# Splitting the pair's combine around the activation transposes, and two neighbouring rows of w_down to a partition

## What is computed

```
gates = softmax over the top 4 of 32 router logits, 0 elsewhere
for each expert e:
    hdn = x @ w_up[e] + b_up[e]                   # 1024 -> 2048
    gt  = min(hdn[:, :1024], 7)
    up  = clip(hdn[:, 1024:], -7, 7)
    act = (up + 1) * gt * sigmoid(1.702 * gt)
    acc += gate[:, e] * (act @ w_down[e] + b_down[e])   # 1024 -> 1024
h = h + acc
```

## Time and profile before

| | us |
|---|---|
| median of 3 runs | 1397.82 |
| lowest, highest | 1396.66, 1398.46 |
| span of the profiled execution, first to last instruction | 1394.0 |
| PE busy in it | 1257.9 |
| the 33 expert passes, from 246.7 to 1300.6 and the last one behind it | to about 1337 |

### The profile page before, as it was taken

How to read it: one execution, slowest core, us unless ns; L and a number is a source line. 1 busy time by engine, 2 the same in 40 slices (tenths; PEclk the granted TensorE clock), 3 DMA queues, 4 the chain that set the end, 5 groups by cost and what they waited for, 6 DMA issues and landing times.

```text
span 1394.0 us, 15526 instructions
## 1 busy us (share of the span) xinstructions
PE 1257.9 (90%) x5839; PEld 604.8 (43%) x5839; DVE 373.9 (27%) x700; ACT 182.2 (13%) x338; POOL 98.6 (7%) x214
## 2 busy tenths in 40 slices
PE   4988898899999999898999999999999899989885
PEld 3645576343434343443434343434344443434254
DVE  6899514121111112121211111111122121120122
ACT  2113403001101010101010110101010101010022
POOL 4565200000000000000000000000000000000000
PEclk8997999899999999999999999999999999998988
DMA  9331213789999999999999999999999999998600
GB/s 313 108 126 60 77 56 129 296 328 407 394 388 386 403 378 397 384 401 377 398 364 383 393 381 400 386 397 379 402 371 406 384 393 377 374 364 347 240 1 32
DMA packets 89134, 438.45 MB, mean 315 GB/s; under 512 B 13616, under 2 KB 16816, under 8 KB 55264
## 3 DMA queue, kind: packets, MB, share of 16 engines
q1 hardware_dynamic: 88528, 437.60, 78.4%
q10 hardware_dynamic: 576, 0.45, 0.1%
HBM read 436.65 MB, written 2.41 MB: 315 GB/s over the span
## 4 chain that ended last, share of the span: by engine, by line
PE 85%; DVE 9%; issue 3%; ACT 2%; DMA 0%; ACTq 0%; DVEq 0%; SPq 0%
PE ps L907 37%; PE ps L923 17%; PE ps L893 10%; PE ps L863 6%; PE ps L797 2%; PE ps L1033 2%; PE ps L914 2%; PE ps L511 2%; PE ps L866 1%; PE ps L591 1%; DVE region L1683 1%; DVE region L1686 1%; DVE region L1680 1%; PE ps L556 1%; PE ps L976 1%
## 5 line engine op out<-in xcount | busy, mean ns | idle before, releaser
L907 PE MATMUL ps<-ring_up,region 128*64 128x512 f32 x2112 | 461.8, 595 | 2.9 <-issue 1.6
L907 PEld LDWEIGHTS ps<-ring_up,region 128*64 128x64 f32 x2112 | 163.4, 137 | 283.3 <-issue 281.4
L923 PE MATMUL ps<-ring_dn,region 128*64 128x512 f32 x1056 | 240.3, 608 | 12.4 <-issue 11.0
L1679 DVE TENSOR_SCALAR region<-ps 128x512 f32<-128x512 f32 x33 | 22.8, 692 | 701.6 <-PE ps L907 701.6
L923 PEld LDWEIGHTS ps<-ring_dn,region 128*64 128x64 f32 x1056 | 82.3, 140 | 157.1 <-issue 155.0
L893 PE MATMUL ps<-region,n_tok 128*128 128x128 f32 (+1 forms) x768 | 136.1, 307 | 0.0
L893 PEld LDWEIGHTS ps<-region,n_tok 128*128 128x128 f32 (+1 forms) x768 | 104.2, 187 | 41.2 <-issue 12.2
L1222 ACT ACTIVATE region<-region 128x512 f32<-128x512 f32 x33 | 20.8, 629 | 499.7 <-DVE region L1679 499.7
L863 PE MATMUL ps<-region 128*128 128x512 f32 (+1 forms) x136 | 80.2, 744 | 2.6 <-issue 1.3
L478 POOL COPY region<-kst 128x64 f32 (+1 forms) x33 | 7.8, 238 | 1040.6 <-PE ps L907 1040.6
L1234 ACT ACTIVATE region<-ps 64x512 f32<-64x512 f32 x66 | 39.1, 592 | 320.7 <-PE ps L923 320.3
(11 more groups left out here) (354 smaller groups left out, 888.2 us busy)
## 6 DMA issues: line engine op xcount, KB each, us to landing
ring_up<-in_w_up_dram SPq DMA_DIRECT2D x264, 1024.0 KB, 11.2
ring_dn<-in_w_down_dram SPq DMA_DIRECT2D x132, 1024.0 KB, 7.0
ring_up<-in_w_in_dram SPq DMA_DIRECT2D x4, 1280.0 KB, 9.9
ring_dn<-in_w_out_dram SPq DMA_DIRECT2D x1, 4096.0 KB, 26.3
ring_up<-in_w_ple_gate_dram SPq DMA_DIRECT2D x4, 1024.0 KB, 6.4
x_tok<-in_x_prompt_dram SPq DMA_DIRECT2D x2, 512.0 KB
ring_up<-in_w_glu_dram SPq DMA_DIRECT2D x1, 1024.0 KB, 16.2
region<-in_w_ple_proj_dram SPq DMA_DIRECT2D x1, 1024.0 KB
```

The source lines that it names most:

```text
L907: m = mm(ps[64 * (q % 2):64 * (q % 2) + 64, q // 2, :], xe[:, k, slots] if k < UP else one_hot, w, start=(k == 0), stop=(k == UP))
L923: m = mm(ps[64 * half:64 * half + 64, O_B, :], act_t[:, f % 4, 64 * (f // 4):64 * (f // 4) + 64], ring_dn[:, f, 512 * half:512 * half + 51 ...
L1679: V.tensor_scalar(g_lim, bank(0), LIMIT, None, ALU.min).then_inc(Z["g_rdy"], 1)
```

## The change

Chunks 0 and 2 of the previous pair's combine go ahead of `turn_activations(t)`, right behind `up(t)`; chunk 1, which uses the banks that the activation is read from, stays behind the transposes. The order of chunks becomes 0, 2, 1 everywhere: in `shares`, in DVE's `added`, and in the counts that ACT's squares behind the experts wait for. And a partition gets two neighbouring rows of `w_down`, 8 KB that lie together; so that the activation's transposes match, they take every second column of `act_v` (the view `by_row`), a step of 8 bytes where it was 4.

```diff
-            dn_w = A["w_down"][0].rearrange("e (s k p) n -> e s p k n", p=P, k=2)
+            dn_w = A["w_down"][0].rearrange("e (s p k) n -> e s p k n", p=P, k=2)
...
-            def shares(weights, outputs, rows_=slice(0, P)):
+            def shares(weights, outputs, rows_=slice(0, P), chunks=(0, 2, 1)):
-                for c, (t0, nt) in enumerate(CHUNKS):
+                for c in chunks:
+                    t0, nt = CHUNKS[c]
...
             def turn_activations(t):
                 pe.wait_ge(Z["act_rdy"], t + 1)
+                by_row = act_v.rearrange("p (s n k) -> p s k n", s=2, k=2)
                 for j in range(4):
-                    m = tr(ps[:, T_B, j * P:(j + 1) * P], act_v[:, j * P:(j + 1) * P], ident)
+                    m = tr(ps[:, T_B, j * P:(j + 1) * P], by_row[:, j // 2, j % 2], ident)
...
-            def combine(p):
+            def combine(p, chunks=(0, 2, 1)):
                 pe.wait_ge(Z["dn_sb"], 2 * p + 2)
                 pe.wait_ge(Z["gt_sb"], p + 1)
-                shares(g_t, lambda half: out_e[:, half])
+                shares(g_t, lambda half: out_e[:, half], chunks=chunks)
...
                 up(t, slice(0, C))
+                if place != "first":
+                    combine(p - 1, (0, 2))
                 turn_activations(t)
                 if place != "first":
-                    combine(p - 1)
+                    combine(p - 1, (1,))
                 down(t)
...
-                act.wait_ge(Z["cmb_read"], (n_visits + PAIRS) * 4 + (1, 2, 4)[c])
+                act.wait_ge(Z["cmb_read"], (n_visits + PAIRS) * 4 + (1, 4, 3)[c])
...
-                for c, (t0, nt) in enumerate(CHUNKS):
-                    dve.wait_ge(Z["cmb_ps"], 3 * n_ + c + 1)
+                for i, c in enumerate((0, 2, 1)):
+                    t0, nt = CHUNKS[c]
+                    dve.wait_ge(Z["cmb_ps"], 3 * n_ + i + 1)
```

## The result

| | median us | lowest, highest | ratio to before, 95% interval |
|---|---|---|---|
| before | 1397.66 | 1396.66, 1398.46 | |
| changed | 1345.48 | 1345.01, 1346.77 | 0.963 [0.962, 0.964] |

The changed kernel is 52.2 us faster; 1335.6 us was forecast, a gain of 62. The profiled execution has a span of 1343.4 us, 50.6 less than before. Some lines have moved: `up` is L908 (was L907), the transposes L916 (L914), `down` L925 (L923), chunks 0 and 1 of the combine L864 (L863), chunk 2 L867 (L866), the activation's last instruction L1691 (L1686).

A forecast was written before the change was run, and what follows sets the result against it. PE was taken to bound the kernel, idle before each pair's transposes and slow-clocked behind; 1394.0 − 63.4 + 1.2 = 1331.8 us of span, plus 3.8 to the median, gave 1335.6 us, range 1329 to 1350 for 8 in 10.

The forecast's parts named there:

- the likeliest case: Whole kernel: 1336 us give or take 6, with a chance of 0.71.
- costly loads: Strided weight loads of the activation's transposes take up to twice a load: 16 us more, 1352 us; chance 0.13.
- What bounds the kernel: Loop over pairs: PE idles 2.8 us before the transposes, and the slow clock behind costs about 1.7 us.
- the forecast's 63.4 us: From first transposes to `down`, 15 pairs: 97.3 us before, 33.9 after, gap filled and clock at 1.00.
- The size of what goes into the gap: Ahead of the transposes: chunk 0's 1.77 us and chunk 2's 0.91, together 2.68 us against 2.83 idle.
- The strided transposes: All 132 activation transposes load every second element: put at 0, bounded above by 16 us.
- rival 3: Clock falls elsewhere, at the 0.7 us idle before the second `down`: up to 1361 us; chance 0.08.
- The sum: Whole kernel: span 1394.0 − 63.4 + 1.2 = 1331.8 us; with the median 3.8 us over the span, 1335.6.
- The stream: Weight DMA in the loop keeps up with pairs of 60.5 us, needing 59.8 to 60.4: put at 0 us.
- Behind the experts: After the loop, ACT's square of chunk 1 waits for the last read: +1.2 us, once.
- The signs in the profile: Two full transpose waits, clock 1.00 through pairs, pairs of 60.5 us, no DMA waits, 33,792 fewer packets under 8 KB.

The follow-up runs named there:

- the split alone: The changed kernel with the old layout of w_down and the old transposes without a step, so only the combine is split: 1338.0 us, ratio 0.957.
- the filled kernel: The kernel before, with a copy of chunks 0 and 2, read by nobody, ahead of the transposes and the combine whole behind them: 1378.5 us, ratio 0.985.
- the kernel whose pairs are 59.67: The changed kernel with half of the gather behind the second transposes, the old layout of w_down and transposes without a step: 1323.6 us, ratio 0.949.
- the layout alone: The kernel before, with the new layout of w_down and the strided transposes, combine as before: 1397.0 us, ratio 1.001.

## Why the prediction was right, and where it was off

**The range held, in part by luck.** 1345.5 us lies within 1329 to 1350, but above the likeliest case, 1336 give or take 6. The upper end of the range had been set for costly loads, up to 16 us of them; they cost 3.0, and most of what was missing came from the clock.

**What bounds the kernel, and the two gains.** Right, and shown separately: with the gap filled by useless work the kernel gains 19 us, which is the clock; taking that work off the path as well (the split alone) gains another 40. In the forecast's 63.4 us the first is 14 x 1.7 = 24; a pair of the filled kernel is 64.86 − 63.24 = 1.6 us shorter, in 13 pairs, and in pair 15 the clock fell at another place.

**The size of what goes into the gap** was short: 2.92 us, not 2.68. I had halved the time of eight like instructions and left out that PE loses about 0.1 us at each change between full-width and half-width matmuls (`128*128` and `128*64` in the rows), of which there are now more: chunk 0 took 640.69 − 638.78 = 1.91 us for 1.77, chunk 2 took 641.70 − 640.69 = 1.01 for 0.91. It cost nearly nothing here, because 2.92 us is just about the wait. It does behind the transposes, where chunk 1 takes 644.09 − 642.28 = 1.81 us for 1.77 and `down` itself lasts 7.09 us, where it was 7.04. With the transposes starting some 0.02 us later that is about 0.12 us a pair, 15 x 0.12 = 1.8 us.

**The strided transposes** were put at 0, with 16 us as the bound. They cost 0.09 us a turn, 3.0 us in all, so the term was mis-sized by the step that chose 0 because 8 bytes are "far nearer to side by side". The load itself did become 209 / 140 = 1.5 times as long, about DVE's factor of 1.4 that had been set aside; what kept the price small is that most of the longer load is hidden. The Trainium skill (Advanced Engine Details and Errata, SBUF Cachelines) wants at least two hits on a 16-byte line and puts a penalty on a different line per access. The runs differ from it: 8 bytes, with two hits, cost 0.09 us too, and 16 bytes, with one, no more than that.

**The clock falling elsewhere** was rival 3, with 0.08, for exactly the place where it happened, the idle time before the second `down`. As rivals the two stood apart, but they came together: the step adds 0.09 us to a stretch where PE does little, and only kernels with the step lost the clock there in pairs 1 to 14 (7 falls in 42 pairs, none in 70 without it), while with the 0.7 us of idle time filled no pair of 14 lost it even with the step. So no kernel here lost the clock there without both. But the step also makes the pair 0.18 us longer, 60.85 us for 60.67, and filling the gap makes it 59.85; no run has the one change without the other. Whether the step and the gap themselves decide or the length of the pair that comes of them is open, and so is by what measure the chip decides. In the profiled run the falls cost 3 x 1.7 us in second halves and 1.7 in pair 15, whose `up` begins at half clock behind the waits of the visit list (before, pair 15 lost the same 1.7 us behind its gap): 6.8 us.

**The sum.** Forecast span 1331.8, measured 1343.4. The difference is 1.8 (changes of width) + 3.0 (step) + 6.8 (clock) = 11.6 us. Between the medians it is 9.9 us, since the median now lies 2.1 us above the profiled span, where 3.8 had been taken over from before.

**The stream.** Right. 414 GB/s in a pair is above what the loop moved before, so its 388 was SP waiting for free places, as argued; and the estimate of 60.4 us for 4 KB runs against 59.8 shows in the kernel whose pairs are 59.67, where their landings fall behind. The Trainium skill's limit of 358 GB/s from HBM for a core (DMA: Bandwidth & Descriptors, Specifications), given there as half of what a stack moves for two cores, does not hold for this kernel on its one core: 420 GB/s over 800 us.

**Behind the experts.** Right. From the visit's `up` to the end it was 93.4 us and is 94.5; +1.2 was forecast. ACT's last two squares in the changed kernel now come one behind the other, where one had run beside DVE's adds:

```profile
1286.83 1.06 ACT L1257 ACTIVATE n_tok<-x_tok 128x1024 f32<-128x1024 f32 x1 [1.70 <-DVE x_tok L1676]
...
1287.89 1.04 ACT L1257 ACTIVATE n_tok<-x_tok 8x1024 f32<-8x1024 f32 x1
```

**The signs in the profile** that the prediction named came out: two full waits left, 72,238 packets with 33,792 fewer under 8 KB, and no wait for weights. The granted clock was not 1.00 through the pairs, as expected, but fell in three; the stretch at 0.50, which was to lie ahead of the second `down` for rival 3, begins 0.4 us behind its start (369.90 and 369.52 us in pair 1), just behind the idle time.

## What to carry to other kernels

An engine's idle time in a loop is to be priced twice, by itself and by what the clock does behind it; independent work that is waiting anyway, cut to the length of the gap, takes back both, and even useless work took back the second. Before a layout is changed for the DMA's sake, look whether anyone waits for the DMA; here nobody did, and the step that the layout forced on the weight loads was its only effect on the time. Check after such an edit where the next smaller gap lies: 0.7 us before the second `down` were worth another 19 us.

## What was not expected of the hardware

A transpose's weight load with a step of 8 or of 16 bytes between float32 columns took the same time more: 209 and 212 ns for 140 at the median, and four transposes 0.58 us for 0.49 with either step. And the clock's falls were regular: in the two traces of the changed kernel three of the four distances between falls in the pairs are 184.3 us, and in the two kernels whose clock falls in each pair (the one before, and the layout alone) the pairs come to 64.85 us, though the second has 0.18 us more to do. Why is not shown.
